# HGRN outputs with tokens in the rows, and their head norm on VectorE, in an encoder layer on one core

## The reference

```python
# HGRN, each direction d, each head: o = (masked scores) @ v + (scaled q) @ state
y_b = o[forward] + flip(o[backward])
y_b = y_b * rsqrt(mean(y_b**2 over the 128 values of a head) + 1e-5) * gnorm_w * gate
x   = x + concat([y_a, y_b]) @ w_out
h2  = rms_norm(x, norm2_w)
x   = x + hier_moe(h2)          # the router reads h2
```

## Time and profile before

| | |
|---|---|
| median of 3 runs | 2420.37 us |
| the runs | 2418.71 to 2426.70 us |
| span of the profiled execution | 2423.5 us (no time of its own is given beside it) |
| TensorE busy | 2270.7 us, 94% |
| VectorE busy | 1029.3 us, 42% |
| ScalarE busy | 719.8 us, 30% |
| GpSimd busy | 420.8 us, 17% |
| the stage of the change | 1236 to 1670 us |

### The profile page before, as it was taken

One profiled execution on the slowest core, in us unless ns is written; L12 is line 12 of the kernel. 1 busy time (PEld: TensorE's weight loads), 2 busy tenths in 40 slices (PEclk: granted clock), 3 DMA queues, 4 the chain that ended last, 5 costly groups with the idle time before them and its releaser, 6 DMA issues. The chain is left out here.

```text
span 2423.5 us, 64808 instructions
## 1 busy us (share of the span) xinstructions
PE 2270.7 (94%) x28110; PEld 1486.5 (61%) x28110; DVE 1029.3 (42%) x2175; ACT 719.8 (30%) x1446; POOL 420.8 (17%) x520
## 2 busy tenths in 40 slices
PE   7989999989999999999979888995899999999997
PEld 4444544445555555555556656753788888888883
DVE  3236777634745645545645645443111111111115
ACT  4224554434544534434522322221000000000003
POOL 1002222200000000000022100012433333333331
PEclk9999999999999999999979888997899999999999
DMA  4113443533342442432365733251899999999986
GB/s 137 35 50 129 134 152 122 191 71 90 90 124 66 117 99 65 116 99 67 113 200 180 214 107 112 81 184 48 325 359 360 333 355 334 356 332 358 363 309 226
DMA packets 359836, 436.48 MB, mean 180 GB/s; under 512 B 164896, under 2 KB 296112, under 8 KB 351408
## 3 DMA queue, kind: packets, MB, share of 16 engines
q1 hardware_dynamic: 343232, 397.94, 48.3%
q0 software_dynamic: 14256, 35.04, 5.8%
q10 hardware_dynamic: 2112, 0.01, 0.1%
HBM read 329.87 MB, written 102.93 MB: 179 GB/s over the span
## 5 line engine op out<-in xcount | busy, mean ns | idle before, releaser
L1188 PE MATMUL h_pp<-hT,r_wcol 128*128 128x512 f32 x832 | 414.9, 622 | 8.8 <-ACT h_iraw L1316 8.8
L2763 PE MATMUL e_ps_gu<-e_xT,e_wg 128*128 128x128 f32 x2048 | 236.4, 277 | 18.5 <-DVE e_xT L2838 18.5
L2763 PEld LDWEIGHTS e_ps_gu<-e_xT,e_wg 128*128 128x128 f32 x2048 | 233.6, 194 | 19.0 <-DVE e_xT L2838 19.0
L2763 PEld LDWEIGHTS e_ps_gu<-e_xT,e_wu 128*128 128x128 f32 x2048 | 233.6, 192 | 14.8 <-issue 14.8
L2763 PE MATMUL e_ps_gu<-e_xT,e_wu 128*128 128x128 f32 x2048 | 233.8, 275 | 0.0
L2772 PE MATMUL e_ps_y<-e_wd,e_hid 128*128 128x512 f32 x512 | 225.1, 592 | 1.1 <-DVE e_hid L2852 1.1
L1188 PEld LDWEIGHTS h_pp<-hT,r_wcol 128*128 128x128 f32 x832 | 142.2, 190 | 130.8 <-issue 110.1
L514 PE MATMUL h_pp<-hT,r_wcol 128*128 128x512 f32 x480 | 209.0, 593 | 1.3 <-DVE hT L784 1.3
L2845 DVE TENSOR_SCALAR e_y<-e_ps_y,e_row 128x512 f32<-128x512 f32 x32 | 24.0, 751 | 336.5 <-PE e_ps_y L2772 325.3
L2772 PEld LDWEIGHTS e_ps_y<-e_wd,e_hid 128*128 128x128 f32 x512 | 94.8, 190 | 108.5 <-issue 108.5
L514 PEld LDWEIGHTS h_pp<-hT,r_wcol 128*128 128x128 f32 x480 | 90.1, 190 | 109.8 <-issue 108.1
(11 more groups left out here) (392 smaller groups left out, 3465.9 us busy)
## 6 DMA issues: line engine op xcount, KB each, us to landing
e_wg<-in_moe_w_gate_dram SPq DMA_DIRECT2D x32, 2048.0 KB
e_wu<-in_moe_w_up_dram SPq DMA_DIRECT2D x32, 2048.0 KB, 14.4
e_wd<-in_moe_w_down_dram SPq DMA_DIRECT2D x32, 2048.0 KB
r_wcol<-in_w_in_dram SPq DMA_DIRECT2D x35, 512.0 KB, 4.8
ar<-r_ar SPq DMA_DIRECT2D x24, 512.0 KB, 2.7
kb<-r_kb SPq DMA_DIRECT2D x24, 512.0 KB, 2.8
m_ar<-ar SPq DMA_DIRECT2D x48, 256.0 KB, 4.6
m_kb<-kb SPq DMA_DIRECT2D x48, 256.0 KB, 3.5
```

Source lines behind the costliest of these rows:

```text
L1188: last = nc.tensor.matmul(pp[n % 2][:], wcol[(k + 2) % 3][:, c], self.hT[:, c, span(s)], start=c == 0, stop=c == KT - 1)
L2763: last = nc.tensor.matmul(ps[:, q * P:(q + 1) * P], w[u][:, c, q * P:(q + 1) * P], xT[u][:, c * P:(c + 1) * P], start=c == 0, stop=c == KT ...
```

## The change

HGRN outputs are formed with tokens in the rows: in `out` the stationary and the moving operand change places. The scores of direction 1 are written mirrored in chunks, and so are its mask and its scaled q, so that both directions leave PSUM in token order, and the copies lose their reversal. A head's channels now lie along a row, so the sum of squares is a `tensor_reduce` on VectorE, as for RWKV. VectorE multiplies the values by the inverse root; TensorE transposes the product; and one VectorE instruction multiplies it by the norm's weight and the gate on the way out of PSUM. Removed are TensorE's `n_ss`, ScalarE's spread copy and VectorE's second gating product. The scaling of q is two instructions instead of one. In the fillers the cost of the HGRN `n_ss` falls from 0.9 to 0. Cut to its core:

```diff
                 norm("n_sq", 0)
-                norm("n_ss", 0, 0.9)
+                norm("n_ss", 0)
...
-                    norm("n_ss", n + 1, 0.9)
+                    norm("n_ss", n + 1)
...
+            def chunk(n, d):
+
+                first = (NC - 1 - n if d else n) * CH
+                return slice(first, first + CH)
...
# TensorE
-                                nc.tensor.matmul(ps_s[r, g, r], kq(c)[:, 0, g, r], kq(c)[:, 1, g, r], start=True,
+                                nc.tensor.matmul(ps_s[r, g, chunk(n, d)], kq(c)[:, 0, g, r], kq(c)[:, 1, g, r], start=True,
...
-                            nc.tensor.matmul(ps_o[:, j], v[u][:, d, j * P:(j + 1) * P], pt[u][:, g], start=True, stop=False)
-                            last = nc.tensor.matmul(ps_o[:, j], state[(c + 1) % 2][:, g], qs[u][:, g], start=False, stop=True)
+                            nc.tensor.matmul(ps_o[:, j], pt[u][:, g], v[u][:, d, j * P:(j + 1) * P], start=True,
+                                             stop=False)
+                            last = nc.tensor.matmul(ps_o[:, j], qs[u][:, g], state[(c + 1) % 2][:, g], start=False, stop=True)
...
-                    def n_ss(k):
-                        if not is_r(k):
-                            self.waits(eng, act_sq.at("sq", k), bank_y.free(("ss", k)))
-                            for i in range(PAIRS):
-                                last = nc.tensor.matmul(ps_y[:, i:i + 1], sq[k % 2][:, i * P:(i + 1) * P], self.allsum[:, 0:1],
-                                                        start=True, stop=True)
-                            last.then_inc(bank_y.made, 1)
...
# ScalarE
-                    def n_inv(k):
-                        if not is_r(k):
-                            self.waits(eng, dve_inv.at("inv", k), bank_x.full(("wide", k - 2)))
-                            nc.scalar.activation(by_k(wide[k % 2][:]), var[k % 2][:, 0:PAIRS].unsqueeze(2).broadcast_to(
-                                (P, PAIRS, P)), ACT.Copy).then_inc(*act_wide.inc("wide"))
...
# VectorE
+                        def scale_q():
+
+                            for d in range(2):
+                                g = by_dir(d)
+                                last = nc.vector.tensor_tensor(
+                                    by_chunk(qs[u][:, g])[:, :, WAY[d]], by_chunk(kq(c)[:, 1][:, g]),
+                                    upto[:, g, c].unsqueeze(3).broadcast_to((P, PAIRS, NC, CH)), ALU.mult)
+                            last.then_inc(*dve_s.inc("q"))
...
+                        self.waits(eng, act_sq.at("sq", k))
+                        nc.vector.tensor_reduce(r, sq[k % 2][:].rearrange("p (h n) -> p h n", n=width), AX_X, ALU.add
+                                                ).then_inc(*dve_var.inc("sumsq"))
+                        self.waits(eng, dve_var.at("sumsq", k))
+                        nc.vector.tensor_scalar(r, r, 1.0 / width, small, ALU.mult, ALU.add).then_inc(*dve_var.inc("var"))
...
+                        if not is_r(k):
+                            nc.vector.tensor_tensor(by_k(wide[k % 2][:]), hgrn(FINISHED[k - ITEMS]),
+                                                    r.unsqueeze(2).broadcast_to((P, PAIRS, P)), ALU.mult
+                                                    ).then_inc(*dve_wide.inc("wide"))
...
-                            nc.vector.scalar_tensor_tensor(rows, rows, gn[:], by_k(ps_x[:]), ALU.mult, ALU.mult
+                            nc.vector.scalar_tensor_tensor(rows, by_k(ps_x[:]), gn[:], by_k(gt[u][:]), ALU.mult, ALU.mult
                                                            ).then_inc(bank_x.read, 1)
-                            nc.vector.tensor_tensor(rows, rows, by_k(gt[u][:]), ALU.mult).then_inc(*dve_h.inc("gated"))
```

More of the change, by code:

```diff
@@ L1794, in mix_hgrn_project_out @@
             dve_r = Marks(self.sem("o_dve_rwkv"), "bonus gated")
-            dve_h = Marks(self.sem("o_dve_hgrn"), "gated")
+            dve_wide = Marks(self.sem("o_dve_hgrn_wide"), "wide")
             pe_out = Marks(self.sem("o_pe_out"), "out")
@@ L1966, in _ @@
                         for d, sign in ((0, 1), (1, -1)):
-                            m = mask[r, d, r]
+                            m = mask[r, d, chunk(q, d)]
                             nc.gpsimd.affine_select(out=m, in_=m, compare_op=ALU.is_ge, fill=0.0,
@@ L1971, in _ @@
                             if q:
-                                nc.gpsimd.memset(mask[r, d, 0:q * CH], 0.0).then_inc(filled, 1)
+                                nc.gpsimd.memset(mask[r, d, (NC - q) * CH:] if d else mask[r, d, 0:q * CH], 0.0
+                                                 ).then_inc(filled, 1)
                     pool.wait_ge(filled, FILLED)
@@ L2031, in load_g @@
                             back = k - RING_G
-                            self.waits(sp, dve_r.at("gated", back) if is_r(back) else dve_h.at("gated", back - ITEMS))
+                            self.waits(sp, dve_r.at("gated", back) if is_r(back) else gated_h(back - ITEMS))
                             sp.dma_start(by_k(gt[u][:]), self.hgate[:, :, tile(t)].rearrange("j p t -> p j t")
@@ L2195, in half @@
                                 self.waits(eng, (wout_loaded[1], 16 * PAIRS), act_r.at("half0", EARLY - 1))
-                            self.waits(eng, dve_r.at("gated", n), dve_h.at("gated", n), dve_x.ago("x1", n, 1))
+                            self.waits(eng, dve_r.at("gated", n), gated_h(n), dve_x.ago("x1", n, 1))
                         for k in range(part * PAIRS, (part + 1) * PAIRS):
@@ L2220, in rank @@
                         self.rank(eng, g, ps_y).then_inc(bank_y.made, 1)
[L2221 removed]
+                    schedule(scores=scores, turn_k=turn_k, grow=grow, out=out, n_wide=n_wide,
                              r_half=r_half, half=half, turn=turn, routed=routed, rank=rank)
@@ L2234, in out @@
                                        dve_x.at("x1", FIRST_OUT.index(t)) if t in FIRST_OUT else None)
-                            rows = hgrn(t)
-                            if d:
-                                rows = rows.rearrange("p j (c k) -> p j c k", k=CH)[:, :, ::-1]
-                                got = ps_o[:].rearrange("p j (c k) -> p j c k", k=CH)
-                            else:
-                                got = ps_o[:]
-                            nc.scalar.activation(rows, got, ACT.Copy).then_inc(bank_o.read, 1)
+                            nc.scalar.activation(hgrn(t), ps_o[:], ACT.Copy).then_inc(bank_o.read, 1)
                     def n_sq(k):
-                        self.waits(eng, dve_var.ago("sumsq", k, 2) if is_r(k - 2) else bank_y.full(("ss", k - 2)))
+                        self.waits(eng, dve_var.ago("sumsq", k, 2))
                         if is_r(k):
```

58 lines of the change are left out of this document (19 added, 39 removed).

## The result

The changed kernel takes 2432.78 us (median of 20 runs, 2428.65 to 2437.21); the kernel before, run beside it, 2424.84 us (20 runs, 2418.07 to 2437.59). The ratio is 1.0031, its 95% interval 1.0021 to 1.0041: slower by 7.5 us, 5.1 to 9.9 (the two medians lie 7.9 apart). The forecast was 7.3 us slower, on a base that was then 4.5 us lower.

A forecast was written before the change was run, and what follows sets the result against it. TensorE's in-order queue in the stage from 1236 to 1670 us was taken as the bound. Legs summed to +6.5 us, +6.8 with the split and +7.3 with the clock, on 2420.4: 2427.7 us, range 2421 to 2434.

The forecast's parts named there:

- the direct edits: Sums, copy and second gating product go; VectorE gains 0.68 us per tile; splitting q's scaling costs 0.3 us in all.
- the rest is hidden: Splitting q's scaling costs 0.3 us over twelve chunks, at the first ones; its other cost does not reach the path.
- x1 behind the scaling: Tiles 2 and 4: x1 at H (output matmuls done) + 6.4, T (h2 transposes) at H + 11.6 us; +5.0 and +5.7.
- Cover gone before T1 and T3: Scan output and state update move behind the h2 transposes: waits at tiles 1 and 3 shorten by 3.0 and 3.1 us.
- Transposes behind transposes: Rounds 1 to 5: the router's second transposes share the norm's PSUM bank and wait for gating, 1.01 us five times.
- Clock: Longer TensorE idle times lower its granted clock in the stage: 0.5 us taken, bounds 0 and 6.5.
- T1 to H2: From tile 1's first h2 transposes to what follows tile 2's last output matmul on TensorE: +1.5 us.
- the clock rival: The clock falls further after TensorE's long idle times in the stage: +10 us, 2438; chance 0.10.
- T0: Start of tile 0's first h2 transposes on TensorE: 0.9 us earlier, as x1 no longer stands behind VectorE's gating.
- TensorE's queue simply gets shorter: Rival: the sums and their waits go from the stage, up to 14.3 + 14.2 us, giving 2392; chance 0.12.
- Gains and losses cancel: Rival: the order's effects cancel, leaving only the last four sums and the split of q's scaling, 2418; chance 0.10.
- The last tiles: Sums of tiles 8 to 11: three go whole, the fourth counts 0.25 us; gain 2.65 us.

The follow-up runs named there:

- keep_order: The changed kernel with the fillers' cost of the HGRN n_ss back at 0.9, so new arithmetic in the old order: 0.9986 of the kernel before, 2423.83 us.
- x1_ahead: The changed kernel with prep of two later chunks held back on VectorE, so x1 of tiles 2 and 4 precedes the scalings: 1.0013 of the kernel before, 2431.05 us.
- order_alone: The kernel before with only the cost of the HGRN n_ss changed, 0.9 to 0: 1.0046 of the kernel before, 2438.76 us.
- items_norm: keep_order with the head norm of tile 0 taken into the pipeline of the twelve RWKV items: 0.9964 of the kernel before, 2420.91 us.

## Why the prediction was right

**The bound and the direct edits.** TensorE's queue in the stage sets the end: right, every verdict above follows TensorE's idle time there. That the early sums hide behind the h2 chain is shown by keep_order: up to H5 it gained nothing. The reduction and the product on VectorE take 679 and 692 ns for the 0.68 and 0.69 that were priced; the pair of scalings 1.29 us against 1.22 in the earlier trace rows, 0.07 a chunk for the 0.1 taken. That "the rest is hidden" was not tested by itself.

**x1 behind the scaling.** Right to 0.1 us at both tiles: x1 at H + 6.3, then 5.2 to T; x1_ahead shows the cause of half of the wait. **Cover gone before T1 and T3.** Right to 0.1 us. **Transposes behind transposes.** The five waits are 0.93 to 0.94 us, and order_alone has them as well (4.7 us in all); no run took them away alone.

**Clock.** Right in sum, wrong in place, and that the whole sum came out so near is luck in part: of the legs above, those longer than forecast are so by 3.7 us together, those shorter by 4.05. The forecast had 0.5 us for the clock in all; the legs T1 to H2 and T3 to H4 came out 1.7 and 0.9 us above it. Behind the wait of 2.80 us the granted clock is 0.50, the 1.2 GHz level, and stays there while the scan's output runs:

```profile
1445.00:1448.00 3.00, 3.00 (x17) 3.00 (x16) 0.10 (x1) 0.69 (x2) 0.00 (x0) 0.50 0.44 175
```

```profile
1444.84 0.52 PE L2169 MATMUL o_ps_o<-e_wu,e_wd 128*128 128x128 f32 x2
1448.15 1.17 PE L2159 MATMUL o_ps_k<-e_wu,e_wg 128*128 128x128 f32 x8
```

The scan output's eight matmuls take 3.31 us, and 1.79 at full clock (from 1458.46 to 1460.25 us in the changed kernel). "After the wait before T1 the sums still ran at full speed" was the argument against the clock rival, and here it failed: that wait was 2.03 us, this one 2.80. It was a weak argument from the start, since a wait of the same 2.03 us before T2 was followed by a clock of 0.50. T0 to H1 came out 0.6 above the forecast, and 0.5 of it is the output matmuls behind T0 (5.21 us against 4.72). In return T2 to H3 and T4 to H5 came out 1.2 and 1.6 us below the forecast, since before these ran at the lower clock too: the eight output matmuls behind T2 take 5.68 us before and 4.52 after, and from 1510.83 to H5 TensorE takes 6.02 us before, 1.67 more than the same transposes and output matmuls take after:

```profile
1510.83 1.07 PE L2145 MATMUL o_ps_k<-ident,e_wd 128*128 128x128 f32 x4
```

The clock rival (+10 us) did not come, as the long waits hit stretches that were slow already. The Trainium skill, TensorE: Matmul & The Clock Gate, Loop structure matters more than you think, warns of such waits; the rows agree in direction, and the size had to be read leg by leg.

**T0.** Here the forecast was wrong by 0.5 us in the leg, and it missed a mechanism: on VectorE the norm of tile 0 stands behind the gating of item 11, which waits 2.46 us for a load. Before, TensorE made the sums in that time. Now reduction and product both come behind it, and the transposes start 2.1 us after the gating instead of 1.3. items_norm shows that this queue holds TensorE up.

**The rivals.** "TensorE's queue simply gets shorter" fell with H to T of 11.5 us, where it wanted under 7. "Gains and losses cancel" fell with the two detours at their full price. The last tiles gained 4.3 us and not 3.3: the five groups of sums there took 0.87 and four times 0.81 us, and all went whole, also the one priced at 0.25.

**Behind the stage.** Forecast as shifted by the same. From the last router matmuls to the first expert matmul it took 37.4 us before and 35.9 after. Of this 1.5 us 1.33 lie at one place, VectorE's wait at the border between two program blocks, of before and of the changed kernel:

```profile
1673.93 0.16 DVE L1604 TENSOR_REDUCE q_gmax<-logits 128x2 f32<-128x8 f32 x1 [3.69 <-PEq L1959]
```

```profile
1683.86 0.16 DVE L1604 TENSOR_REDUCE q_gmax<-logits 128x2 f32<-128x8 f32 x1 [2.36 <-PEq L1964]
```

## What to carry to other kernels

A matmul that sits in front of a wait may cost nothing: ask what TensorE does next and when that is ready, before pricing its removal. Where a planner sets the order from costs, changing a cost is an edit of its own, and worth a kernel of its own (the cost alone here: 11 us slower; the arithmetic alone: 3 us faster, by its interval 0 to 7). Look on every engine for what stands ahead of the step that TensorE waits for: here five scalings on VectorE, a load's wait on VectorE, and a square on ScalarE each held up a short step that had its inputs, and moving each was worth as much as the arithmetic in the order of before or more (by the middle values 4, 5 and 37 us against 3; the intervals of the first two overlap with those that they are compared with).

## What was not expected of the hardware

The stretch behind the stage, 37.3 to 37.7 us, in the three programs with the old arithmetic, is 35.9 to 36.6 us in the ten traces with the new, though no instruction in it changed. VectorE's wait at the border of the two blocks, 3.69 us before and 2.36 after, is 3.69 to 4.07 us in the three and 2.31 to 3.04 in the ten, and GpSimd's is shorter by 0.85 us at the same place (before against after). What makes it shorter was not tried and stays open.
